# A routing stage rebuilt: squares and weighted rows on TensorE, row arithmetic on GpSimd, row scaling inside the first expert pass

## The chip, the cores and the metric

One NeuronCore of a Trainium2 chip runs the whole program. The metric is the device time of one execution in microseconds (us). Before the change it is 1565.91 us, the median of three runs (1565.65 to 1567.62).

## What is computed

336 tokens (16 meta, 256 prompt, 64 sample) of 1024 channels go through two layers. Each layer is a token mixer followed by a channel mixer; in layer 1 the channel mixer sends every token to two of eight experts:

```
hn = rmsnorm(h, norm2_g)
top_val, top_idx = top_k(hn @ router_w, 2);  gates = softmax(top_val)
y = sum over e of combine[:, e] * ((silu(hn @ wg[e]) * (hn @ wu[e])) @ wd[e])
h = h + y
```

The change lies between the end of the token mixer of layer 1 and the first expert. What has to be known there: the eight router logits of each token, `1/rms` of each token, the two chosen experts, the rank of the token among those of its expert (its row in that expert's chunk of 128 rows), the normalised rows themselves, and the two gates.

## The kernel before

**Layout.** Up to the routing, activations lie with channels on partitions: `h` is 128 x 8 x 336 (eight groups of 128 channels). For the experts, tokens are gathered into chunks of 128 rows. A product of full precision is done as three matmuls in a reduced type (`mm3`, L1571 to L1573) on a high and a low part of both operands. Every weight tile of 1 MB lands in one of six `raw` buffers (SP issues the loads), ScalarE copies it to the high part `w_hi` (L509, "the split"), VectorE subtracts that to get the low part `w_lo` (L514), and TensorE uses both; `w_hi` and `w_lo` have three buffers each, so the split of tile i waits until TensorE is done with tile i-3.

**Output projection of layer 1 (`wout`).** Eight groups of 24 matmuls, two per weight tile; VectorE adds each to `h` (L1321). In between TensorE computes the router's logits of finished channel groups (L1795: three matmuls per channel group, eight columns each), turns the states for output (L1654), and turns `h` to tokens on partitions by transposition (`htok`, L1827: channels 0 to 511 after group 5, the rest after group 7).

**Routing.** VectorE finds the two best experts (L1411 on), `hot` marks them, TensorE sums `hot` over earlier tokens to get ranks (L1882, L1884). ScalarE copies the second half of the turned rows out of PSUM (L999) and sums their squares (L992); VectorE multiplies the rows by the norm's weight (`hn`, L1426) and computes `1/rms` (L1082 on). `sel` (L1443) is the 0/1 matrix of the first expert's rows times `1/rms`; 24 matmuls with `hn` (L1894) gather the first expert's rows straight into PSUM banks `X0`, `X1`; ScalarE and VectorE split those to `xg_hi` (L1013) and `xg_lo` (L1492). For the other seven experts, ScalarE scales all rows by `1/rms` (`hs`, L1006; its buffer shows as `og`), VectorE computes each row's number (L1434 to L1470), and GpSimd scatters the rows to `xg` in DRAM by six indirect DMAs (L734); SP loads each chunk from there in the pass before it is wanted (L573), the first time only after GpSimd's `x_rows`.

**Expert passes.** A loop of eight passes over 42 weight tiles each ("slots"): gate 0 and 1, up 2 and 3, gate of the next block 4 and 5, and so on; 12 matmuls per slot. After slot 1 ScalarE applies Silu (L1031). SP issues the load of slot i when `w_lo` of slot i-6 is done.

What sets the order is the order of the code on each engine, and semaphores between engines. GpSimd's operations of one chain wait for each other (`link`).

Of the kernel before, what the change touches and what calls it, by code (L numbers as in the profile page):

```python
# [22 lines left out]
def hybrid_trunk(nc, x_prompt, x_sample, state_pool, state_conv, meta_tokens, norm1_g, w_in, pool_w,  # L23
# [38 lines left out]

    PE_TAPS = (TAPS, TAPS, TAPS - 1)
# [43 lines left out]
    for l in range(L):  # L107
# [7 lines left out]
        for m in range(KD):  # L115
            plan(("wout", l, m))
            if l == 1 and m == STATE_AFTER:
                plan(*[("state", l, i) for i in range(5)])
            if l == 1 and m in HALF_DONE:

                plan(*[("htok", t, HALF_DONE.index(m)) for t in range(3)])
# [12 lines left out]
    with ExitStack() as ctx:  # L134
# [95 lines left out]
        prod = sb("prod", [TT, 3, 2, NE], F32, moe)  # L230
# [27 lines left out]
        table_load = sb("table_load", [1, 1], F32, moe)  # L258
# [4 lines left out]
        TAP_BANK, N_TAPS = ps[:, 6, 0:L * KC * TAPS], L * KC * TAPS  # L263
        G_, U_, T_, X0, X1 = (ps[:, i, :] for i in (0, 1, 2, 5, 6))
# [32 lines left out]
        gb_landed, hn_sq = sem("gb_landed"), sem("hn_sq")  # L297
# [3 lines left out]
        routed, extra_done = sem("routed"), sem("extra_done")  # L301
# [89 lines left out]


# [127 lines left out]
        def _(sp):  # L520
# [29 lines left out]
            def load_expert(p, e):  # L550
                for j in range(NJ):
# [4 lines left out]
                    for i, w, half, jj in todo:  # L556
# [12 lines left out]
                        if i == gate_slot(2):  # L569
# [38 lines left out]
        def _(pool):  # L608
# [119 lines left out]

            pool.wait_ge(filled, 16 * (2 * CHUNKS + 1))
# [10 lines left out]
            pool.wait_ge(routed, 1)  # L740
# [30 lines left out]
            pool.wait_ge(out_rows_done, 1)  # L771
# [50 lines left out]
        def _(act):  # L822
# [18 lines left out]
            def mixer_layer(l):  # L841
# [153 lines left out]
            token_squares(og[:, 0], [(t, 0) for t in range(3)], lambda t, i: act.wait_ge(evac, GROUP[("htok", t, 0)] + 1), hn_sq)  # L995
            act.wait_ge(evac, GROUP[("htok", 0, 1)])
# [12 lines left out]
            def gathered_hi(p):  # L1009

                for i, x in enumerate((X0, X1)):
                    act.wait_ge(gather_done, p * 2 + (i + 1))
                    nc.scalar.activation(xg_hi[:, 4 * i:4 * i + 4, :], x.rearrange("p (k s) -> p k s", k=4), ACT.Copy  # L1013
                                         ).then_inc(xg_hi_done, 1)
# [8 lines left out]
            def expert_pass(p):  # L1023
# [16 lines left out]
                nc.scalar.activation(table_load[:], ones[0:1, 0:1], ACT.Silu)  # L1040
                for i in range(ES):
                    split_hi_pass(act, p, i)
                    if i == 0:
                        gathered_hi(p)
                    else:
                        after(i - 2)

            with act.Fori(0, NE) as p:
# [16 lines left out]
        def _(dve):  # L1065
# [347 lines left out]
            for t in range(3):  # L1413
# [595 lines left out]
```

## Time and profile before

| | |
|---|---|
| time, median of three | 1565.91 us |
| the profiled execution | 1565.94 us |
| its span (first to last instruction) | 1564.2 us |
| TensorE busy | 1516.5 us (97%) |
| VectorE / ScalarE / GpSimd busy | 1226.7 / 997.5 / 155.4 us |
| HBM traffic | 421.60 MB read, 25.12 MB written |

Times in the views are counted from the span's start. 1.74 us of the profiled execution lie around the span. The output projection of layer 1 ends at about 549 us, the first expert matmul starts at 570.00 us. A "busy" TensorE is one with a matmul in flight: matmuls overlap, so the step from one start to the next says what one costs. A matmul on plain fp32 data shows as two records.

### The profile page before, as it was taken

How to read it: one execution, taken by the hardware profiler on the slowest of the kernel's cores; microseconds unless marked ns; L12 is line 12 of the kernel's file. 1: busy time of each engine (PE TensorE's matmuls, PEld its weight loads, DVE VectorE, ACT ScalarE, POOL GpSimd, SP SyncE). 2: the span in 40 equal slices, each digit the busy share in tenths (PEclk: the TensorE clock that was granted, in tenths of full speed). 3: DMA queues.
4: the chain of work that ended last, by engine and by line, in shares of the span. 5: the costliest groups of instructions: out<-in, count | busy, mean ns of one | idle time of the engine just before them, and what ended most of it. 6: DMA issues, size and time to landing. Idle time of an engine off the chain costs nothing.

```text
span 1564.2 us, 21646 instructions
## 1 busy us (share of the span) xinstructions
PE 1516.5 (97%) x7897; PEld 1321.2 (84%) x7897; DVE 1226.7 (78%) x1053; ACT 997.5 (64%) x1018; POOL 155.4 (10%) x209
## 2 busy tenths in 40 slices
PE   7999999999998989999999999999999999999995
PEld 7989999999998977788888888888888888888884
DVE  4797755544498578888888888888888888888887
ACT  5765343333584267777777777777777778777773
POOL 1036200002122237000000000000000000000002
PEclk9999999999999989999999999999999999999998
DMA  6233998343133449999999999999999999999993
GB/s 194 88 129 115 304 303 253 108 142 128 54 115 108 153 171 394 383 366 392 365 364 386 373 363 379 371 369 382 367 363 372 380 367 366 386 359 367 392 367 105
DMA packets 243536, 447.40 MB, mean 286 GB/s; under 512 B 8901, under 2 KB 93957, under 8 KB 243487
## 3 DMA queue, kind: packets, MB, share of 16 engines
q1 hardware_dynamic: 239296, 436.83, 78.4%
q0 software_dynamic: 2960, 9.73, 2.0%
q8 instruction: 30, 0.49, 0.1%
q10 hardware_dynamic: 1231, 0.19, 0.1%
q14 instruction: 19, 0.16, 0.0%
HBM read 421.60 MB, written 25.12 MB: 286 GB/s over the span
## 4 chain that ended last, share of the span: by engine, by line
issue 57%; PE 4%; POOL 3%; DVE 2%; DMA 2%; ACT 1%; DVEq 0%; POOLq 0%; ACTq 0%
PE ps L1571 1%; PE ps L1573 1%; PE ps L1572 1%; POOL og L767 1%; DMA xg<-og,row_i 1%; POOL h L758 1%; POOL xg L734 0%; DMA h<-last_row 0%; DMA last_row<-last_pos 0%; DMA og<-obuf,out_row_i 0%; POOL pick L754 0%; POOL h L726 0%; DVE scratch L1171 0%; DVE y L1173 0%; PE ps L1795 0%
## 5 line engine op out<-in xcount | busy, mean ns | idle before, releaser
L514 DVE TENSOR_TENSOR w_lo<-raw,w_hi 128x2048 fp32r<-128x2048 f32 x336 | 769.5, 2292 | 126.9 <-ACT w_hi L509 125.3
L509 ACT ACTIVATE w_hi<-raw 128x2048 fp32r<-128x2048 f32 x336 | 643.5, 1916 | 133.9 <-PE ps L1573 122.2
L1571 PE MATMUL ps<-w_hi,xg_hi 128*128 128x512 f32 x896 | 354.9, 396 | 2.5 <-DVE xg_lo L1492 1.6
L1572 PE MATMUL ps<-w_lo,xg_hi 128*128 128x512 f32 x896 | 353.6, 395 | 0.0
L1573 PE MATMUL ps<-w_hi,xg_lo 128*128 128x512 f32 x896 | 353.6, 395 | 0.0
L1571 PEld LDWEIGHTS ps<-w_hi,xg_hi 128*128 128x128 f32 x896 | 168.5, 188 | 43.6 <-DVE xg_lo L1492 1.8
L1573 PEld LDWEIGHTS ps<-w_hi,xg_lo 128*128 128x128 f32 x896 | 168.6, 188 | 40.1
L1572 PEld LDWEIGHTS ps<-w_lo,xg_hi 128*128 128x128 f32 x896 | 168.7, 188 | 39.2
L1571 PE MATMUL ps<-x_hi,w_hi 128*128 128x336 f32 x580 | 187.7, 324 | 10.1 <-DVE x_lo L1117 3.8
L1573 PE MATMUL ps<-x_hi,w_lo 128*128 128x336 f32 x580 | 185.5, 320 | 0.0
L1572 PE MATMUL ps<-x_lo,w_hi 128*128 128x336 f32 x580 | 185.2, 319 | 0.0
L1571 PE MATMUL ps<-w_hi,ft_hi 128*128 128x512 f32 x448 | 181.2, 405 | 0.0
L1573 PE MATMUL ps<-w_hi,ft_lo 128*128 128x512 f32 x448 | 177.1, 395 | 0.0
L1572 PE MATMUL ps<-w_lo,ft_hi 128*128 128x512 f32 x448 | 176.7, 394 | 0.0
L502 DVE TENSOR_TENSOR w_lo<-raw,w_hi 128x2048 fp32r<-128x2048 f32 (+3 forms) x41 | 85.1, 2079 | 55.3 <-ACT w_hi L484 53.9
L1571 PEld LDWEIGHTS ps<-x_hi,w_hi 128*128 128x128 f32 x580 | 110.6, 191 | 14.2 <-issue 6.1
L1572 PEld LDWEIGHTS ps<-x_lo,w_hi 128*128 128x128 f32 x580 | 110.7, 191 | 0.3
L1573 PEld LDWEIGHTS ps<-x_hi,w_lo 128*128 128x128 f32 x580 | 110.4, 190 | 0.0
L484 ACT ACTIVATE w_hi<-raw 128x2048 fp32r<-128x2048 f32 (+3 forms) x41 | 70.1, 1719 | 53.7 <-PE ps L1573 53.7
L1573 PEld LDWEIGHTS ps<-w_hi,ft_lo 128*128 128x128 f32 x448 | 84.2, 188 | 19.7
L767 POOL DMA_INDIRECT og<-obuf,out_row_i x6 | 11.5, 1920 | 889.2 <-SPq L595 887.7
L1572 PEld LDWEIGHTS ps<-w_lo,ft_hi 128*128 128x128 f32 x448 | 84.5, 189 | 17.6
(275 smaller groups left out, 1871.2 us busy)
## 6 DMA issues: line engine op xcount, KB each, us to landing
raw<-in_moe_w_gate_dram SPq DMA_DIRECT2D x112, 1024.0 KB, 7.6
raw<-in_moe_w_up_dram SPq DMA_DIRECT2D x112, 1024.0 KB, 7.9
raw<-in_moe_w_down_dram SPq DMA_DIRECT2D x112, 1024.0 KB, 7.5
raw<-in_w_in_dram SPq DMA_DIRECT2D x11, 1024.0 KB, 5.0
raw<-in_ffn_w_gate_dram SPq DMA_DIRECT2D x11, 1024.0 KB, 5.9
raw<-in_ffn_w_up_dram SPq DMA_DIRECT2D x11, 1024.0 KB, 6.4
raw<-in_w_out_dram SPq DMA_DIRECT2D x8, 1024.0 KB, 5.1
obuf<-ones SPq DMA_DIRECT2D x15, 512.0 KB, 7.9
```

The lines of the kernel that those rows point to most:

```text
L484: nc.scalar.activation(hi, r, ACT.Copy).then_inc(hi_done, 1)
L502: nc.vector.tensor_tensor(lo, r, hi.bitcast(F32), ALU.subtract).then_inc(lo_done, 1)
L509: nc.scalar.activation(hi, r, ACT.Copy).then_inc(hi_done, 1)
L514: nc.vector.tensor_tensor(lo, r, hi.bitcast(F32), ALU.subtract).then_inc(lo_done, 1)
L758: link(nc.gpsimd.tensor_tensor(pick_e[:, i, NE * c:NE * (c + 1)], pick[:, i, NE * c:NE * (c + 1)], iota_e[:], ALU.mult))
L767: nc.gpsimd.indirect_dma_start(out=og[:, i, t, :], out_offset=None, in_=obuf, in_offset=bass.IndirectOffsetOnAxis(ap=out_row_i[:, i, t:t + ...
L1571: nc.tensor.matmul(out, a_hi, b_hi, start=start, stop=False)
L1572: nc.tensor.matmul(out, a_hi, b_lo, start=False, stop=False)
L1573: return nc.tensor.matmul(out, a_lo, b_hi, start=False, stop=stop)
```

## The change

On TensorE the squares of a channel group, made by ScalarE in its channel layout, are summed over channels by matmuls with a column of ones, three for each of eight channel groups, beside the logits of the same group. The logits of groups 4 and 5 move ahead of the last output group. The second half of `hn` comes from matmuls of `h` with a diagonal matrix of the norm's weight in place of a transposition and a VectorE product; the transposition of the second half stays (the residual needs it) and moves behind the ranks. Four matmuls on constants stand ahead of the gather. ScalarE loads the table for Exp by a one-element instruction ahead of the wait for the gap; the scaling of all rows (`hs`) leaves the routing and stands in pass 0 between the Silu of slot 1 and the split of slot 4; pass 0 is written out and the loop runs over the other seven. Its split of the gathered rows comes one half per slot. The row numbers and the ordering of the two gates go from VectorE to GpSimd, which gets a copy of the ranks in SBUF. On SP, the store of a finished chunk and the load of the next chunk both stand after slot 16, the store first; before, the load stood after slot 10.

TensorE, from the end of the last output group to the first expert matmul, before (`rwg` is the router's weight, `ident` the identity: transposition):

```order
L1573 MATMUL ps<-m_hi,w_lo 128x336
L1795 MATMUL ps<-rwg,h 112x8 x12
L1827 MATMUL ps<-ident,h 112x128 x12
L1882 MATMUL ps<-hot,before 128x32
L1884 MATMUL ps<-hot,ones 128x24
L1884 MATMUL ps<-hot,ones 128x16
L1884 MATMUL ps<-hot,ones 128x8
L1894 MATMUL ps<-sel,hn 128x128 x24
```

and in the changed kernel (`y_pool` holds squares, `z` the diagonal of the weight):

```order
L1603 MATMUL ps<-m_hi,w_lo 128x336
L1835 MATMUL ps<-rwg,h 112x8 x6
L1843 MATMUL ps<-ones,y_pool 112x1 x6
L1874 MATMUL ps<-z,h 112x128 x12
L1677 MATMUL ps<-hot,before 128x32
L1679 MATMUL ps<-hot,ones 128x24
L1679 MATMUL ps<-hot,ones 128x16
L1679 MATMUL ps<-hot,ones 128x8
L1886 MATMUL ps<-ident,h 112x128 x12
L1638 MATMUL ps<-ones,ident 128x128 x4
L1947 MATMUL ps<-sel,hn 128x128 x24
```

Squares and the product with the diagonal stand ahead of the ranks, the transposition behind them; six of the twelve logits matmuls have moved ahead of the last output group, where TensorE now has:

```order
L1835 MATMUL ps<-rwg,h 112x8 x3
L1843 MATMUL ps<-ones,y_pool 112x1 x3
L1835 MATMUL ps<-rwg,h 112x8 x3
L1843 MATMUL ps<-ones,y_pool 112x1 x3
L1601 MATMUL ps<-m_hi,w_hi 128x336
```

The same kind of block stands at the two earlier places, where before six logits matmuls stood.

ScalarE, from its last copies out of the turned rows into the first pass, before:

```order
L999 ACTIVATE yt<-ps 112x512 [waits mm_done] x2
L992 ACTIVATE og,nt<-yt 112x512 [waits evac] x3
L1006 ACTIVATE og<-hn,nt 112x1024 [waits hn_done,gap_done]
L1006 ACTIVATE og<-hn,nt 112x1024 [waits hn_done] x2
L1007 ACT_TABLE_LOAD
L1007 ACTIVATE gt<-gt 112x3
L1048 UNCONDITIONAL_BRANCH
L1040 ACT_TABLE_LOAD
L1040 ACTIVATE table_load<-ones 1x1
```

and in the changed kernel, the routing's end and then the place of the row scaling:

```order
L1065 ACTIVATE yt<-ps 112x512 [waits mm_done] x2
L1067 ACT_TABLE_LOAD
L1067 ACTIVATE table_load<-ones 1x1
L1069 ACTIVATE gt<-gt 112x3 [waits gap_done]
L1100 ACT_TABLE_LOAD
L1100 ACTIVATE table_load<-ones 1x1
L520 ACTIVATE w_hi<-raw 128x2048 [waits w_used,landed0]
```

```order
L520 ACTIVATE w_hi<-raw 128x2048 [waits w_used,landed3]
L1091 ACTIVATE act_s<-ps 128x512 [waits e_f,g_done]
L1111 ACTIVATE og<-hn,nt 112x1024 [waits hn_done]
L1111 ACTIVATE og<-hn,nt 112x1024 x2
L520 ACTIVATE w_hi<-raw 128x2048 [waits g_done,landed4]
```

The three scalings have moved from ahead of the table loads to between the Silu of slot 1 and the split of slot 4.

The diff's core:

```diff
+
+        def squared(k):
+            return scratch[:, k, :] if k < 4 else y_pool[:, k - 4, :]
...
-                        if i == gate_slot(2):
+                        if i == gate_slot(3):
+
+                            sp.wait_ge(o_done, p * 2 + 2)
+                            sp.dma_start(obuf_chunks[ds(p, 1)].rearrange("a p d -> p (a d)"), o[:]
+                                         ).then_inc(o_stored, 16)
...
-                        if i == gate_slot(3):
-
-                            sp.wait_ge(o_done, p * 2 + 2)
-                            sp.dma_start(obuf_chunks[ds(p, 1)].rearrange("a p d -> p (a d)"), o[:]
-                                         ).then_inc(o_stored, 16)
...
+            def fold_experts(x, out):
+
+                for n in (4, 2, 1):
+                    link(nc.gpsimd.tensor_tensor(x[:, :, 0:n], x[:, :, 0:n], x[:, :, n:2 * n], ALU.add))
+                link(nc.gpsimd.tensor_copy(out, x[:, :, 0]))
+
+            def pick_expert(out, values):
+                link(nc.gpsimd.tensor_tensor(prod[:].rearrange("p (t k) e -> p t k e", t=3), hot2[:], values, ALU.mult))
+                fold_experts(prod, out[:].rearrange("p t k -> p (t k)"))
+
+            pool.wait_ge(ranks_copied, 1)
+            pick_expert(rank, ranks_sb[0:TT, 0:3].unsqueeze(2).broadcast_to([TT, 3, 2, NE]))
...
+            fold_experts(before_e, key_e[:])
+            link(nc.gpsimd.tensor_scalar(key_e[:], key_e[:], float(P), None, ALU.mult))
+            link(nc.gpsimd.tensor_tensor(key_e[:], key_e[:], extra_base[:], ALU.add))
+            pick_expert(jump, key_e[0:TT].unsqueeze(1).unsqueeze(1).broadcast_to([TT, 3, 2, NE]))
...
+            link(nc.gpsimd.tensor_tensor(row[:], row[:], jump[:], ALU.add))
+            nc.gpsimd.tensor_copy(row_i[:], row[:]).then_inc(rows_done, 1)
...
+            pool.wait_ge(gates_done, 1)
+            first_row, gap, step_up = row[:, :, 0], last_pos[:], early_gate[:]
+            link(nc.gpsimd.tensor_tensor(gap, first_row, row[:, :, 1], ALU.subtract))
...
+            link(nc.gpsimd.tensor_copy(out_row_i[:], out_row[:]))
+            pool.sem_inc(out_rows_done, 1)
...
+                        continue
+                    if s == 0:
+                        act.wait_ge(evac, GROUP[("wout", 1, 0)] + 1)
+                        for k in range(4):
+                            nc.scalar.activation(z[:, k, P:2 * P], ident[:], ACT.Copy, scale=col(1, NG2, 4 + k)
+                                                 ).then_inc(gain_done, 1)
+                    for k in (2 * s, 2 * s + 1):
+                        act.wait_ge(evac, GROUP[("wout", 1, k)] + 1)
+                        nc.scalar.activation(squared(k), h[:, k, :], ACT.Square).then_inc(h_sq, 1)
...
-            token_squares(og[:, 0], [(t, 0) for t in range(3)], lambda t, i: act.wait_ge(evac, GROUP[("htok", t, 0)] + 1), hn_sq)
-            act.wait_ge(evac, GROUP[("htok", 0, 1)])
+            act.wait_ge(evac, GROUP[("hn", 0)])
+            for t in range(3):
+                act.wait_ge(mm_done, GROUP[("hn", t)] + 1)
+                nc.scalar.activation(hn[:, t, 512:1024], ps[0:TT, GROUP[("hn", t)] % MM_BANKS, :], ACT.Copy
+                                     ).then_inc(hn_turned, 1)
+                act.wait_ge(hn_turned, t + 1)
+                act.sem_inc(evac, 1)
...
-            token_squares(og[:, 0], [(t, 1) for t in range(3)], lambda t, i: act.wait_ge(evac, GROUP[("htok", t, 1)] + 1), hn_sq)
-
+            nc.scalar.activation(table_load[:, 1:2], ones[0:1, 0:1], ACT.Exp)
             act.wait_ge(gap_done, 1)
-            for t in range(3):
-                act.wait_ge(hn_done, 3 + t + 1)
-                nc.scalar.activation(hs[:, t, :], hn[:, t, :], ACT.Copy, scale=nt[0:TT, t, 1:2]).then_inc(hn_scaled, 1)
             nc.scalar.activation(gt[:, :, 1], gt[:, :, 0], ACT.Exp).then_inc(exp_done, 1)
 
...
+                    if i < 2:
+                        gathered_hi(p, i)
...
+                    if i == rows_at:
+
+                        act.wait_ge(hn_done, 3)
+                        for t in range(3):
+                            nc.scalar.activation(hs[:, t, :], hn[:, t, :], ACT.Copy, scale=nt[0:TT, t, 1:2]
+                                                 ).then_inc(hn_scaled, 1)
+
+            expert_pass(0, ROWS_AT)
+            with act.Fori(1, NE) as p:
...
+            dve.wait_ge(squares_done, 1)
+            link(nc.vector.tensor_scalar(nt[0:TT, :, 0], SQUARE_SUMS, 1.0 / D, 1e-6, ALU.mult, ALU.add))
             nc.vector.tensor_tensor(hot[:, 0:3], hot2[:, :, 0, :], hot2[:, :, 1, :], ALU.add).then_inc(hot_done, 1)
             dve.wait_ge(hot_done, 2)
...
-            for t in range(3):
-                dve.wait_ge(evac, GROUP[("htok", t, 1)] + 1)
-                nc.vector.tensor_tensor(hn[:, t, 512:1024], yt[:, t, 512:1024], gb[:, 0, 512:1024], ALU.mult
-                                        ).then_inc(hn_done, 1)
-            dve.wait_ge(hn_sq, 6)
-            rstd_tokens()
-            link(nc.vector.tensor_tensor(gt[:, :, 0], top[:, :, 1], top[:, :, 0], ALU.subtract))
...
+            rsqrt(nt[0:TT, :, 0], nt[0:TT, :, 1], nt[0:TT, :, 2], nt[0:TT, :, 3])
...
+            link(nc.vector.tensor_tensor(gt[:, :, 0], top[:, :, 1], top[:, :, 0], ALU.subtract))
+            nc.vector.tensor_tensor(gt[:, :, 0], gt[:, :, 0], nt[0:TT, :, 1], ALU.mult).then_inc(gap_done, 1)
+            nc.vector.tensor_copy(ranks_sb[:].rearrange("p t e -> p (t e)"), ps[:, 7, 0:4 * NE]).then_inc(ranks_copied, 1)
...
-            pick_expert(rank, ps[0:TT, 7, 0:3 * NE].rearrange("p (t e) -> p t e", t=3).unsqueeze(2)
-                        .broadcast_to([TT, 3, 2, NE]))
...
-            nc.vector.tensor_copy(row_i[:], row[:]).then_inc(rows_done, 1)
-
-            dve.sem_inc(routed, 1)
...
+            nc.vector.tensor_tensor(gt[:, :, 3], gt[:, :, 1], gt[:, :, 2], ALU.mult).then_inc(gates_done, 1)
...
+                def token_squares(k):
+
+                    pe.wait_ge(h_sq, k + 1)
+                    for t in range(3):
+                        ins = nc.tensor.matmul(SQUARE_SUMS[:, t:t + 1], squared(k)[:, TT * t:TT * (t + 1)],
+                                               ones[:, 0:1], start=(k == 0 and t == 0), stop=(k == KD - 1 and t == 2))
+                    return ins
...
+                        if l == 1 and s and i == (0 if s == 3 else 1):
+                            for k in (2 * s - 2, 2 * s - 1):
+                                logits(k)
+                                token_squares(k)
                     m = 2 * s + 1
-                    if l == 1 and s:
-                        for k in (m - 3, m - 2):
-                            logits(k)
                     if l == 1 and m == KD - 1:
                         logits(KD - 2)
                         logits(KD - 1).then_inc(logits_done, 1)
+                        token_squares(KD - 2)
+                        token_squares(KD - 1).then_inc(squares_done, 1)
+                        pe.wait_ge(gain_done, 4)
+                        for t in range(3):
+                            out = group(("hn", t))
+                            for k in range(4):
+                                ins = nc.tensor.matmul(out[0:TT, P * k:P * (k + 1)], h[:, 4 + k, TT * t:TT * (t + 1)],
+                                                       z[:, k, P:2 * P], start=True, stop=True)
+                            ins.then_inc(mm_done, 1)
+                        ranks()
                     if l == 1 and m == STATE_AFTER:
...
-            pe.wait_ge(hn_done, 6)
+            keep_busy(WARM_ROUTE, 6)
+            pe.wait_ge(hn_done, 3)
+            pe.wait_ge(hn_turned, 3)
             pe.wait_ge(sel_ready, 3)
```

## Rows read from the trace of the kernel before

**Rows 1.** Timeline of TensorE: start us, us, engine, line, operation, count [idle before <-releaser].
```profile
549.18 2.43 PE L1795 MATMUL ps<-rwg,h 128*112 128x8 f32 x24
551.47 1.79 PE L1827 MATMUL ps<-ident,h 128*112 128x128 f32 x12
553.69 1.43 PE L1884 MATMUL ps<-hot,ones 112*128 112x24 f32 x6
559.64 8.72 PE L1894 MATMUL ps<-sel,hn 112*128 112x128 f32 x48 [4.53 <-DVE sel L1443]
570.00 0.50 PE L1571 MATMUL ps<-w_hi,xg_hi 128*128 128x512 f32 x1 [1.64 <-DVE xg_lo L1492]
```

**Rows 2.** Windows: stretch, PE PEld DVE ACT POOL busy, granted clock, DMA, GB/s.
```profile
700.00:1500.00 800.00, 800.00 (x3565) 649.30 (x3564) 695.95 (x384) 596.03 (x407) 0.00 (x0) 1.00 1.02 372
```

**Rows 3.** Waits of TensorE from 569 to 700 us: total, times, longest.
```profile
PE ps L1571 <- DVE xg_lo L1492: 1.6, 1, 1.6
PE ps L1571 <- DVE w_lo L514: 0.9, 3, 0.4
```

**Rows 4.** Timeline of TensorE in layer 0: sums over channels of one column.
```profile
110.65 2.43 PE L1768 MATMUL ps<-ones,z 128*112 128x1 f32 x24
```

**Rows 5.** Timeline of VectorE around the routing and the first slots.
```profile
549.38 0.51 DVE L1321 TENSOR_TENSOR h<-h,ps 128x336 f32<-128x336 f32 x1 [3.20 <-PE ps L1573]
567.05 2.29 DVE L514 TENSOR_TENSOR w_lo<-raw,w_hi 128x2048 fp32r<-128x2048 f32 x1
569.26 1.28 DVE L1492 TENSOR_TENSOR xg_lo<-ps,xg_hi 128x512 fp32r<-128x512 f32 x2
578.77 4.61 DVE L514 TENSOR_TENSOR w_lo<-raw,w_hi 128x2048 fp32r<-128x2048 f32 x2 [1.07 <-ACT w_hi L509]
```

**Rows 6.** Windows of the gather (L1894) alone: PE, PEld busy, clock, DMA, GB/s.
```profile
560.00:564.00 4.00, 4.00 (x20) 4.00 (x20) 0.50 0.00 0
566.20:568.40 2.20, 2.16 (x19) 1.97 (x18) 1.00 0.64 199
```

**Rows 7.** Timeline of ScalarE: scaling, table loads, splits.
```profile
558.36 3.23 ACT L1006 ACTIVATE og<-hn,nt 112x1024 f32<-112x1024 f32 x3 [2.64 <-DVE gt L1431]
561.61 1.28 ACT L1007 ACT_TABLE_LOAD   x1
564.53 1.89 ACT L509 ACTIVATE w_hi<-raw 128x2048 fp32r<-128x2048 f32 x1
576.83 1.91 ACT L509 ACTIVATE w_hi<-raw 128x2048 fp32r<-128x2048 f32 x1
```

**Rows 8.** Timeline of TensorE: first matmuls of slots 1 and 4.
```profile
573.25 0.49 PE L1571 MATMUL ps<-w_hi,xg_hi 128*128 128x512 f32 x1 [0.21 <-DVE w_lo L514]
581.72 0.39 PE L1571 MATMUL ps<-w_hi,xg_hi 128*128 128x512 f32 x1
```

**Rows 9.** Windows: the granted clock (ahead of DMA) at four places.
```profile
57.60:61.00 3.40, 3.40 (x17) 3.40 (x16) 3.29 (x4) 2.40 (x2) 0.00 (x0) 0.50 0.00 0
61.00:64.40 3.40, 3.40 (x28) 3.40 (x27) 3.29 (x5) 0.34 (x1) 0.00 (x0) 1.00 0.48 140
528.60:531.80 3.20, 3.20 (x33) 3.10 (x32) 1.96 (x4) 0.00 (x0) 0.46 (x1) 1.00 0.02 9
552.50:566.20 13.70, 9.17 (x44) 8.71 (x43) 10.87 (x50) 10.99 (x17) 0.96 (x1) 0.50 0.01 2
```

**Rows 10.** Timeline of GpSimd: scatter and first arithmetic.
```profile
565.24 1.05 POOL L734 DMA_INDIRECT xg<-og,row_i  x1 [29.45 <-DVE row_i L1470]
583.47 0.58 POOL L742 TENSOR_SCALAR over<-cnt 128x8 f32<-128x8 f32 x2 [7.34 <-DMA xg<-og,row_i]
584.14 2.15 POOL L743 TENSOR_TENSOR n_chunks<-over 128x8 f32<-128x8 f32 x1
```

**Rows 11.** Timeline of SP: the load of slot 16.
```profile
598.01 0.37 SPq L568 DMA_DIRECT2D raw<-in_moe_w_gate_dram  x1
```

**Rows 12.** The page's DMA issues: KB each, median us to landing.
```profile
raw<-in_moe_w_gate_dram SPq DMA_DIRECT2D x112, 1024.0 KB, 7.6
```

More of the change, by code:

```diff
@@ L61, in hybrid_trunk @@
     WARM = (12, 10)
+    WARM_ROUTE = 4
+    ROWS_AT = 3
     PE_TAPS = (TAPS, TAPS, TAPS - 1)
@@ L119, in hybrid_trunk @@
             if l == 1 and m in HALF_DONE:
+                if m == KD - 1:
+                    plan(*[("hn", t) for t in range(3)])
                 plan(*[("htok", t, HALF_DONE.index(m)) for t in range(3)])
@@ L296, in hybrid_trunk @@
         state_stored = sem("state_stored")
-        gb_landed, hn_sq = sem("gb_landed"), sem("hn_sq")
+        gb_landed, h_sq, gain_done = sem("gb_landed"), sem("h_sq"), sem("gain_done")
+        squares_done, ranks_copied, gates_done, hn_turned = (
+            sem(n) for n in ("squares_done", "ranks_copied", "gates_done", "hn_turned"))
         rwg_done, logits_done, hot_done, ranks_done = sem("rwg_done"), sem("logits_done"), sem("hot_done"), sem("ranks_done")
@@ L769, in gather_outputs @@
                     in_offset=bass.IndirectOffsetOnAxis(ap=out_row_i[:, i, t:t + 1], axis=0)).then_inc(done, 16)
-            pool.wait_ge(out_rows_done, 1)
+            pool.wait_ge(gates_done, 1)
+            first_row, gap, step_up = row[:, :, 0], last_pos[:], early_gate[:]
+            link(nc.gpsimd.tensor_tensor(gap, first_row, row[:, :, 1], ALU.subtract))
+            for i, under in enumerate((ALU.is_lt, ALU.is_ge)):
+                link(nc.gpsimd.tensor_scalar(lower[:, i, :], gap, 0.0, None, under))
+            link(nc.gpsimd.tensor_tensor(step_up, gap, lower[:, 0, :], ALU.mult))
+            link(nc.gpsimd.tensor_tensor(out_row[:, 0, :], row[:, :, 1], step_up, ALU.add))
+            link(nc.gpsimd.tensor_tensor(out_row[:, 1, :], first_row, step_up, ALU.subtract))
+            for i in (0, 1):
+                link(nc.gpsimd.tensor_tensor(out_gate[:, i, :], lower[:, i, :], gt[:, :, 2], ALU.mult))
+                link(nc.gpsimd.tensor_tensor(part_gate[:, i, :], lower[:, 1 - i, :], gt[:, :, 3], ALU.mult))
+            link(nc.gpsimd.tensor_tensor(out_gate[:], out_gate[:], part_gate[:], ALU.add))
+            link(nc.gpsimd.tensor_scalar(out_row[:], out_row[:], float(P), None, ALU.add))
+            link(nc.gpsimd.tensor_copy(out_row_i[:], out_row[:]))
+            pool.sem_inc(out_rows_done, 1)
             link(nc.gpsimd.tensor_scalar(last_base[:], eids_f[0:TT, 6:7], -float(P), -float(P * NE), ALU.mult, ALU.add))
@@ L1513, in expert_pass @@
                     split_lo_pass(dve, p, i)
-                    if i == 0:
-                        gathered_lo(p)
+                    if i < 2:
+                        gathered_lo(p, i)
                     else:
@@ L1603, in spread, with keep_busy @@
                 nc.tensor.matmul(SUM_BANK, ones[0:TT, :], spread_in, start=True, stop=True).then_inc(sums_done, 1)
-            def keep_busy(n):
+            def keep_busy(n, bank=7):
                 for _ in range(n):
-                    nc.tensor.matmul(ps[:, 7, 0:P], ident[:], ones[:], start=True, stop=True)
+                    nc.tensor.matmul(ps[:, bank, 0:P], ident[:], ones[:], start=True, stop=True)
             pe.wait_ge(consts, 1)
@@ L1641, in split_ready, with ranks @@
                 pe.wait_ge(lo_done, n + 1)
+            def ranks():
+                pe.wait_ge(hot_done, 2)
+                flat = hot[:].rearrange("p t e -> p (t e)")
+                nc.tensor.matmul(ps[:, 7, 0:4 * NE], before[0:TT, :], flat, start=True, stop=False)
+                for t in range(3):
+                    ins = nc.tensor.matmul(ps[:, 7, NE * (t + 1):4 * NE].rearrange("p (u e) -> p u e", e=NE), ones[0:TT, :],
+                                           hot[:, t, :].unsqueeze(1).broadcast_to([TT, 3 - t, NE]), start=False, stop=t == 2)
+                ins.then_inc(ranks_done, 1)
             def turn_states(l):
@@ L1818, in mixer_layer @@
                         logits(KD - 1).then_inc(logits_done, 1)
+                        token_squares(KD - 2)
+                        token_squares(KD - 1).then_inc(squares_done, 1)
+                        pe.wait_ge(gain_done, 4)
+                        for t in range(3):
+                            out = group(("hn", t))
[4 more added lines that the diff above has]
+                        ranks()
                     if l == 1 and m == STATE_AFTER:
@@ L1877, in _ @@
             mixer_layer(1)
-            pe.wait_ge(hot_done, 2)
-            flat = hot[:].rearrange("p t e -> p (t e)")
-            nc.tensor.matmul(ps[:, 7, 0:4 * NE], before[0:TT, :], flat, start=True, stop=False)
-            for t in range(3):
-                ins = nc.tensor.matmul(ps[:, 7, NE * (t + 1):4 * NE].rearrange("p (u e) -> p u e", e=NE), ones[0:TT, :],
-                                       hot[:, t, :].unsqueeze(1).broadcast_to([TT, 3 - t, NE]), start=False, stop=t == 2)
-            ins.then_inc(ranks_done, 1)
-            pe.wait_ge(hn_done, 6)
+            keep_busy(WARM_ROUTE, 6)
+            pe.wait_ge(hn_done, 3)
+            pe.wait_ge(hn_turned, 3)
             pe.wait_ge(sel_ready, 3)
```

72 lines of the change are left out of this document (26 added, 46 removed).

## The prediction

> **What bounds the kernel now.** I read the timeline of TensorE first, between the last group of the output projection and the first expert matmul [rows 1]. The last group ends at 549.18 us, the experts start at 570.00: 20.8 us in which TensorE does little and waits twice, for `sel` (4.53) and for `xg_lo` (1.64). Next the windows behind it: from 700 to 1500 us TensorE is busy in 800.00 of 800 us at full clock [rows 2]; from 569 to 700 its waits come to 1.6 us (`xg_lo`) and 0.9 us (three for `w_lo`, the longest 0.4) [rows 3]. So the experts run at TensorE's pace; what moves the first expert matmul, or adds a wait of TensorE in pass 0, moves the end by as much. The chain of waits at the page's end names other engines; it follows semaphores back and does not say which engine has no time left, so I don't use it.
>
> **TensorE ahead of the last output group.** The squares of six channel groups are 18 matmuls on plain data, 36 records; 12 logits records move to here. A one-column matmul costs what an eight-column one does: 24 records take 2.43 us in layer 0 [rows 4] and 2.43 for the logits [rows 1]. From start to start that is (551.47 - 549.18)/24 = 0.095 us. 48 x 0.095 = **+4.6 us**, all of it between output groups that depend on nothing else, so on the path. The rule that speaks otherwise is in the Trainium skill, "TensorE: Matmul & The Clock Gate", "Back-to-back issue gap": matmuls of up to 64 columns come some 25 ns apart. By it (an estimate) the 48 would take 1.2 us and the sum below would be 3.4 lower. The same page, "LDWEIGHTS", has a weight load take its columns divided by 1.2 in ns, 93 ns at 112 columns, and with that the 0.095 of this trace agrees.
>
> **The tail after that group.** I count from 549.18 + 4.6 = 553.8. Logits of group 6: 0.57. Group 7's wait for VectorE's addition, which in before ends 549.38 + 0.51 - 549.18 = 0.7 us after the group [rows 5]; its logits, to 1.3. Squares of groups 6 and 7, 12 x 0.095, to 2.5. The product with the diagonal has the shape of the gather, 24 records; the gather alone shows 19 records in 2.16 us at full clock, 0.114 each, and 20 in 4.00 at half, 0.2 each [rows 6]. So 2.7, to 5.2. Ranks: 8 records, 0.9, to 6.1. Transposition of 12: between 12 x 0.114 = 1.4 and the 1.79 seen; 1.5, to 7.6. From here ScalarE carries the path: the last copy (half of one 1024-wide scaling, 3.23/3/2 = 0.54) to 8.1; two table loads with their small instructions, which in before last from 561.61 to 564.53, 2.9, and one more small one, 3.0 in all, to 11.1; the split of a weight tile, 1.89, to 13.0 [rows 7]. Then VectorE: `w_lo` 2.29 and half of the two `xg_lo`, 0.64 [rows 5], to 16.0. First expert matmul at 553.8 + 16.0 = 569.8, 0.2 earlier than before. Slot 1 in before waits for `w_lo` until 573.25 [rows 8]; the changed kernel makes that `w_lo` ahead of slot 0, so slot 1 starts near 572.9. I take **-0.3** for both. The gather comes at some 8.5, lasts 48 x 0.114 = 5.5, and is done at 14, ahead of `w_lo`'s end, so its four matmuls on constants cost nothing; that cover ends 2 us later. Bounds: -1.2 if the copy and the small instructions hide beside TensorE, up to +4.1 through the clock.
>
> **The clock.** TensorE's granted clock has two levels, 1.2 and 2.4 GHz. Behind the narrow matmuls and the transposition it is 0.50 of full from 552.5 to 566.2; in layer 0, work that waits runs at 0.50 with 17 records in 3.40 us where 28 fit later at 1.00; 12 narrow records beside transpositions at 528.6 to 531.8 stayed at 1.00 [rows 9]. The changed kernel has four stretches of 24 narrow records, three of them inside the output projection. One stay like the one at 57.6 in full-size matmuls costs 3.40 x (1 - 17/28) = 1.3 us. Nothing of before shows 24 narrow records inside running products, so the cost lies between 0 and, for three stays, 3.9; alternatively the tail runs at half clock: the diagonal product 24 x 0.086 = 2.1, ranks 1.0, transposition 1.0, together 4.1. I take one stay, **+1.3**.
>
> **The row scaling in pass 0.** In before ScalarE splits slot 4 at 576.83 to 578.74 [rows 7], VectorE subtracts from 578.77 to 578.77 + 4.61/2 = 581.07 [rows 5], TensorE wants it at 581.72 [rows 8]: 0.65 us to spare. Three scalings, 3.23 us [rows 7], now stand in front of that split, behind a Silu that itself waits for TensorE. So TensorE waits 3.23 - 0.65 = **+2.6 us** at slot 4. Behind it ScalarE needs 1.9 a slot against TensorE's 2.82 and catches up at once, and all demand is 2.3 us later, while the landings of the weights are not: of the 0.9 us of `w_lo` waits, those after slot 1 (0.9 - 0.2) go, **-0.6**, at worst 0.
>
> **Off the path, costed at nothing.** The chain for the row numbers (27 operations on GpSimd) can start near 562, once the ranks (553.8 + 6.1) are copied and VectorE's `sel` is through; its GpSimd form takes 0.29 us an operation (two in 0.58), and beside a `w_lo` of VectorE 2.15 [rows 10]. The first 14 (0.35 each with a gap) end near 567, before VectorE is loaded again; 13 more at 0.4 to 2.2 end between 572 and 596. The scatter then takes 583.47 - 565.24 = 18.2 us [rows 10], so the rows are there between 598 and 615 (the scaling, done near 580, gives 598 too). SP wants them where the load of the next chunk now stands, behind the load of slot 16, which it asks for at 598.01 [rows 11] + 2.3 = 600.3. Queued behind that wait are the loads of slot 17 on; TensorE goes from slot 1 to slot 4 in 581.72 - 573.25, 2.82 a slot, and comes to slot 17 near 581.7 + 2.3 + 13 x 2.82 = 621, so with 7.6 to land [rows 12] and 4.2 for split and subtraction SP may wait until 609. The Trainium skill, "GPSIMD Engine Reference", "Performance versus the Vector engine", has plain arithmetic about twice as slow there as on VectorE. By it the chain would take some 11 us (an estimate) and SP would not wait; the 2.15 us of the trace is worse than this, and only through it does the rival below have a chance. SP's store of a finished chunk now stands ahead of that wait and is off the path. GpSimd's gate arithmetic serves the end of the kernel, far behind. The VectorE operations that go stood in the 20.8 us, and the path there is counted anew.
>
> **Sum.** -0.3 + 1.3 + 2.6 - 0.6 = +3.0 on the profiled 1565.94: **1568.9**. That this lies 0.03 above the median of the runs is nothing. Of the parts, +4.6 is paid in full by what the tail saves; the gain on paper is spent ahead of it.
>
> **Rivals.**
> 1. *No stay at half clock.* The 528.6 window speaks for it, the 552.5 one against. +1.7: 1567.6.
> 2. *The tail at half clock*, as from 552.5 in before, beside the terms without the stay: 1.7 + 4.1 = +5.8: 1571.7. For it: the same narrow stretch precedes the tail; against: the wait in it is shorter.
> 3. *The row numbers come late*: GpSimd beside VectorE as in the 2.15 us row, all 13 times, SP held until 615: 6 more than the forecast, 1575. It decides if the chain ends after 591; against: VectorE has gaps in pass 0.
> 4. *The scaling is hidden; not slower.* The place is slot 4: if the split of slot 4 is done within its spare 0.65 us (the scalings lie beside a wait that ScalarE has there anyway, as Silu waits for TensorE, or a late landing decides the time of that split), TensorE doesn't wait: -0.9 to +0.4, 1565.0 to 1566.3, and with a start at the bound of -1.2 below 1562.8 when the stays are missing and the narrow records overlap the output groups' weight loads.
> 5. *The 48 narrow records cost 1.2 us*, by the rule named: +3.0 - 3.4, 1565.5; with rival 4 below 1562.8.
>
> **How the numbers follow.** A difference of 0.2%, 3.1 us, is about what a measurement of this kernel can tell from none: the bounds are 1562.8 and 1569.0. Chances: forecast 0.36 (own range 1567.3 to 1570.3; 0.19 of it same, 0.17 slower), rival 1 0.22 (0.20 same, 0.02 slower), rival 2 0.19 (slower), rival 3 0.04 (slower), rival 4 0.15 (0.06 faster, 0.09 same), rival 5 0.04 (0.03 faster, 0.01 same). Together faster 0.09, same 0.49, slower 0.42. The range 1564.3 to 1573.0 leaves out the lower part of rivals 4 and 5 and the upper one of 2 and 3.
>
> **What would show it.** Right: the first expert matmul near 569.8; a wait of TensorE of 2.6 us for `w_lo` at slot 4, with the three scalings between Silu and split on ScalarE; one-column records 0.095 apart; one window at 0.50 among the output groups from 520 to 554; no waits for `w_lo` after slot 4; SP's load of slot 17 behind no wait. Wrong: the diagonal product at 0.2 a record (rival 2), slot 4 on time (rival 4), TensorE waiting near slot 17 with SP held by GpSimd (rival 3).

## The result, and the profile after

The changed kernel takes 1573.06 us, median of seven runs (1572.42 to 1575.13), against 1566.67 us of the kernel before, also of seven (1564.02 to 1568.76). The ratio is 1.0042, with an interval of 1.0032 to 1.0052: 6.4 us slower. A second set of twelve runs beside 35 of before gave 1.0034 (1.0022 to 1.0046). Forecast were 1568.9 us, 3.0 more than before, and a range that ended at 1573.0, with a chance of 0.42 for slower, 0.49 for the same and 0.09 for faster. The sign was right; the loss was about twice the forecast's.

The profiled execution has a span of 1572.2 us, 8.0 more than before. Below, the tail is the stretch from the end of the last output group to the first expert matmul, and a stay is a stretch of some microseconds in which the granted clock is 0.50, the lower of its two levels. The timeline of TensorE in the tail, and the first matmul of slot 4:

```profile
556.22 1.52 PE L1835 MATMUL ps<-rwg,h 128*112 128x8 f32 x12
557.59 1.58 PE L1843 MATMUL ps<-ones,y_pool 128*112 128x1 f32 x12
559.03 4.25 PE L1874 MATMUL ps<-z,h 128*112 128x128 f32 x24
563.93 1.50 PE L1886 MATMUL ps<-ident,h 128*112 128x128 f32 x12
566.16 5.52 PE L1947 MATMUL ps<-sel,hn 112*128 112x128 f32 x48
574.08 0.50 PE L1601 MATMUL ps<-w_hi,xg_hi 128*128 128x512 f32 x1 [2.39 <-DVE xg_lo L1521]
589.41 0.79 PE L1601 MATMUL ps<-w_hi,xg_hi 128*128 128x512 f32 x1 [2.37 <-DVE w_lo L525]
```

Against [rows 1] the tail is shorter, 17.9 us (556.22 to 574.08) for 20.8; the wait for `sel` (4.53 us before) is gone, and the gather takes 5.52 us for 8.72. The tail begins later, though, and the diagonal product takes 4.25 us where 2.7 were forecast. The wait for `xg_lo` is still there, longer than before, and slot 4 has a wait that it did not have [rows 8]. The waits of TensorE from 520 to 700 us, where before had 4.5 for `sel`, 1.6 for `xg_lo` and three for `w_lo` of together 0.9 [rows 1, rows 3]:

```profile
PE ps L1601 <- DVE xg_lo L1521: 2.4, 1, 2.4
PE ps L1601 <- DVE w_lo L525: 2.4, 1, 2.4
```

Windows of the same execution (TensorE, weight loads, VectorE, ScalarE, GpSimd busy, then the granted clock): the output projection, the diagonal product, what follows it, the matmuls behind each of the two waits, and the late passes of [rows 2]:

```profile
516.00:556.20 40.20, 40.20 (x298) 40.09 (x297) 18.24 (x24) 10.76 (x16) 5.21 (x10) 1.00 0.38 125
558.70:562.10 3.40, 3.40 (x18) 3.40 (x19) 2.19 (x13) 0.60 (x1) 0.00 (x0) 0.53 0.00 0
562.10:566.10 4.00, 4.00 (x39) 4.00 (x38) 1.52 (x8) 2.70 (x5) 0.17 (x1) 1.00 0.01 2
575.60:578.90 3.30, 3.30 (x9) 2.63 (x8) 3.30 (x3) 1.48 (x4) 3.05 (x4) 0.50 1.02 366
589.40:592.60 3.20, 3.19 (x8) 2.52 (x9) 3.20 (x3) 1.23 (x1) 2.66 (x2) 0.50 0.48 90
700.00:1500.00 800.00, 800.00 (x3562) 649.28 (x3561) 695.46 (x383) 590.28 (x404) 0.00 (x0) 1.00 1.01 372
```

The late passes are untouched. There are three stays, and none is in the output projection, where the forecast had put its one. ScalarE, the end of the routing and the place of the scaling, to set beside [rows 7]:

```profile
566.19 1.28 ACT L1067 ACT_TABLE_LOAD   x1
567.80 1.28 ACT L1100 ACT_TABLE_LOAD   x1
569.20 1.89 ACT L520 ACTIVATE w_hi<-raw 128x2048 fp32r<-128x2048 f32 x1
582.01 3.22 ACT L1111 ACTIVATE og<-hn,nt 112x1024 f32<-112x1024 f32 x3
585.13 5.50 ACT L520 ACTIVATE w_hi<-raw 128x2048 fp32r<-128x2048 f32 x3
```

GpSimd, beside [rows 10]: the row numbers are ready before the scaled rows, and the scatter waits 6.14 us for ScalarE.

```profile
579.80 0.19 POOL L766 CAST row_i<-row 112x6 int32<-112x6 f32 x1
586.13 1.10 POOL L773 DMA_INDIRECT xg<-og,row_i  x1 [6.14 <-ACT og L1111]
604.94 2.56 POOL L780 TENSOR_SCALAR over<-cnt 128x8 f32<-128x8 f32 x2 [7.29 <-DMA xg<-og,row_i]
```

So the 8.0 us of the spans: 2.3 lie ahead of the change (the output projection begins at 513.74 before and 516.04 after); the projection takes 35.4 and 40.2 us (+4.74); the tail 20.8 and 17.9 (-2.96); and from the first expert matmul to the 240th matmul on gathered rows behind it 82.2 and 86.2 (+4.0). The last three sum to +5.8 us, between the 6.4 and the 5.3 (0.34% of 1567.8) of the timed sets.

### The profile page after: what moved, and what is told of

Read it like the earlier page. It is cut to its first block, busy times and chain, and to the rows that moved or that the text cites. A ratio compares the mean times of both kernels' runs of the same rounds, so it can differ in the third digit from the quotient of the medians.

```text
span 1572.2 us, 21802 instructions
## 1 busy us (share of the span) xinstructions
PE 1527.5 (97%) x7977; PEld 1332.8 (85%) x7977; DVE 1221.3 (78%) x1025; ACT 991.5 (63%) x1015; POOL 189.5 (12%) x249
## 4 chain that ended last, share of the span: by engine, by line
issue 55%; PE 5%; POOL 5%; DVE 2%; DMA 2%; ACT 1%; POOLq 0%; DVEq 0%; ACTq 0%
PE ps L1601 1%; PE ps L1603 1%; PE ps L1602 1%; POOL h L796 1%; POOL og L805 1%; POOL xg L773 1%; DMA xg<-og,row_i 1%; POOL key L784 0%; DMA h<-last_row 0%; DMA last_row<-last_pos 0%; DMA og<-obuf,out_row_i 0%; POOL pick L792 0%; PE ps L1843 0%; DVE scratch L1238 0%; DVE y L1240 0%
```

## The experiments

The theory: the terms that were forecast are there, and to them come stays in the diagonal product and behind each of the two waits of TensorE. Its rivals: the loss lies in code ahead of the change, or late landings decide. All ratios are to the kernel before, timed beside each; an interval of 0.1% either way is 1.6 us, so what a stay costs is read from the profiles and not from the times.

**The scaling on VectorE.**

```diff
-                    if i == rows_at:
-                        act.wait_ge(hn_done, 3)
-                        for t in range(3):
-                            nc.scalar.activation(hs[:, t, :], hn[:, t, :], ACT.Copy, scale=nt[0:TT, t, 1:2]
...
+            def scaled(t):
+                dve.wait_ge(hn_done, 3)
+                dve.wait_ge(hn_turned, t + 1)
+                nc.vector.tensor_scalar(hs[:, t, :], hn[:, t, :], nt[0:TT, t, 1:2], None, ALU.mult).then_inc(hn_scaled, 1)
+            scaled(0)
...
+            scaled(1)
+            scaled(2)
```

> The changed kernel, but VectorE scales the rows by 1/rms, in the time it has between the ranks and the first expert (one tile ahead of the ranks' wait, two behind the gates), and ScalarE's three scalings in pass 0 are gone. Theory (the wait of TensorE at slot 4, 2.37 us in the changed kernel's trace, comes from the 3.22 us of scaling, and the half-clock matmuls from 589 to 593, some 1.5 us, come from that wait): TensorE does not wait at slot 4, its clock stays at 1.00 there, and the time is 3.9 us under the changed kernel's 1573.1: 1569.2. Rival one (the wait goes, but the clock falls there anyway): 2.4 us, 1570.7. Rival two (a late landing decides slot 4): the wait stays, named for the DMA, under 1 us gained.

Ratio 1.0020 (1.0007 to 1.0032), 2.2 to 3.5 us below the changed kernel's 1.0042 and 1.0034 in its own two sets: less than the 3.9 expected, and rival one's 2.4 fits too. The waits of TensorE from 569 to 700 us, and the window 575 to 579:

```profile
PE ps L1603 <- DVE xg_lo L1523: 2.4, 1, 2.4
PE ps L1603 <- DVE w_lo L525: 0.2, 1, 0.2
575.00:579.00 4.00, 3.94 (x17) 3.15 (x18) 4.00 (x4) 3.38 (x4) 3.78 (x4) 1.00 0.82 269
```

The wait at slot 4 is gone and nothing late took its place (the 0.2 us stand at 624), so rival two falls. No stay stands there either (1.00 from 575 to 600), so in this profile rival one falls too. The third row shows something else: behind the same wait for `xg_lo` the clock stayed at 1.00 this time. In this profile two stays came in the output projection instead, which took 43.3 us in place of 40.2; in the other five profiles of kernels with all 48 narrow records there it took 40.1 or 40.2.

**Table loads off the path.**

```diff
+            nc.scalar.activation(table_load[:, 1:2], ones[0:1, 0:1], ACT.Exp)
             act.wait_ge(evac, GROUP[("hn", 0)])
...
-            nc.scalar.activation(table_load[:, 1:2], ones[0:1, 0:1], ACT.Exp)
             act.wait_ge(gap_done, 1)
...
-                nc.scalar.activation(table_load[:, 0:1], ones[0:1, 0:1], ACT.Silu)
+                if rows_at is None:
+                    nc.scalar.activation(table_load[:, 0:1], ones[0:1, 0:1], ACT.Silu)
...
+                        if i == 1 and rows_at is not None:
+                            nc.scalar.activation(table_load[:, 0:1], ones[0:1, 0:1], ACT.Silu)
```

> The changed kernel, but ScalarE loads the table for Exp ahead of its copies out of the turned rows, where it waits for TensorE anyway, and the one for Silu behind the split of slot 1. Theory (between the last copy and the first split two table loads and three small instructions, 3.0 us, stand on the path; without them TensorE begins the experts right behind the gather): the wait for xg_lo, 2.39 us, goes to under 0.3, the half-clock matmuls from 575.5 to 579, 1.1 us, go with it, and the time is 3.5 us under the changed kernel's: 1569.6. Rival one (only the wait goes): 2.4, 1570.7. Rival two (a copy under the table of Exp loads another table, or the split waits for something else): no gain.

Ratio 1.0019 (1.0007 to 1.0031), 2.4 to 3.6 us below the changed kernel's; expected were 3.5, and the 2.4 of the wait alone fit as well. ScalarE, and then the waits of TensorE from 530 to 700 us:

```profile
570.81 0.22 ACT L1069 ACTIVATE gt<-gt 112x3 f32<-112x3 f32 x1
570.91 1.92 ACT L520 ACTIVATE w_hi<-raw 128x2048 fp32r<-128x2048 f32 x1
577.11 1.28 ACT L1107 ACT_TABLE_LOAD   x1
```

```profile
PE ps L1604 <- DVE w_lo L525: 2.9, 2, 2.3
```

The first split follows the small Exp at once, the tail is 15.3 us in place of 17.9, and the wait for `xg_lo` is gone. One of the two waits left is slot 4's, 2.3; the other, 0.56, is new, at slot 2, where the load for Silu now stands ahead of the split. The theory holds for the table loads. That the clock is at 1.00 behind the first expert matmul here says little, as it was so in two of the five profiles that kept the wait.

**Wide sums.**

```diff
-        SQUARE_SUMS = ps[0:TT, 7, 4 * NE:4 * NE + 3]
+        SQUARE_COLS = ps[0:TT, 7, 64:64 + 3 * 64]
+        SQUARE_SUMS = SQUARE_COLS.rearrange("p (t c) -> p t c", c=64)[:, :, 0]
...
-                        ins = nc.tensor.matmul(SQUARE_SUMS[:, t:t + 1], squared(k)[:, TT * t:TT * (t + 1)],
-                                               ones[:, 0:1], ...
+                        ins = nc.tensor.matmul(SQUARE_COLS[:, 64 * t:64 * (t + 1)], squared(k)[:, TT * t:TT * (t + 1)],
+                                               ones[:, 0:64], ...
```

> The changed kernel, but every sum of squares is made 64 times over (a matmul with 64 columns of ones in place of one). Theory (the diagonal product ran at half clock, 4.25 us where 2.7 was forecast, because of what TensorE did right before it, and a matmul of 64 columns costs no more time than one of one): the product takes 2.7 us at clock 1.00 and the time is 1.4 us under the changed kernel's: 1571.7. Rival one (the clock does not follow the matmuls' columns): the product stays at 4.2 us, same time. Rival two (the 48 matmul records get longer): up to 1 us slower.

Ratio 1.0029 (1.0020 to 1.0039). The diagonal product, its window, and the window behind the wait for `xg_lo`:

```profile
557.79 2.83 PE L1875 MATMUL ps<-z,h 128*112 128x128 f32 x24
557.80:560.40 2.60, 2.60 (x26) 2.60 (x26) 2.10 (x13) 1.19 (x2) 0.00 (x0) 1.00 0.02 6
571.50:574.50 3.00, 3.00 (x7) 2.39 (x8) 3.00 (x3) 2.43 (x3) 2.75 (x4) 0.50 0.79 253
```

From its start to the ranks the product takes 2.67 us for 4.09. In the eight profiles with one-column sums it took 4.06 to 4.29, in the three with wide ones 2.66 or 2.67: this stay is no chance, and the columns of the sums right ahead of the product decide it, as nothing else was changed. Rival two falls: the projection takes 40.1 us with 64 columns as with one. The stay behind the wait for `xg_lo` is back here. The interval alone can't tell 1.4 us from nothing; the profiles do.

**Matmuls on constants in the wait.**

```diff
+    WARM_GATHERED = 10
...
                 ins.then_inc(gather_done, 1)
+            pe.wait_ge(ranks_copied, 1)
+            keep_busy(WARM_GATHERED, 7)
```

> The changed kernel with ten matmuls on constants (2.2 us) between the gather and the first expert matmul, where TensorE waited 2.39 us for xg_lo. Theory (the half clock from 575.5 to 579 follows from that wait): the first expert matmul comes when it did, the clock stays at 1.00 through slots 0 and 1, and the time is 1.1 us under the changed kernel's: 1572.0. Rival (the clock falls for another reason, or the wait is harmless): within 0.3 us of the changed kernel.

Ratio 1.0028 (1.0015 to 1.0041). The window behind the first expert matmul (at 577.05, 17.85 us after the last group, as in the changed kernel):

```profile
577.00:580.00 3.00, 2.94 (x13) 2.32 (x14) 3.00 (x4) 2.59 (x3) 2.69 (x5) 1.00 0.80 243
```

The clock is at 1.00, as expected. But of the five profiles with an unfilled wait of 2.39 us it was at half in three, so one filled profile is no proof. The time, 0.9 to 2.2 us below the changed kernel's of the two other sets, can't tell the expected 1.1 from nothing. Inconclusive.

**The changed kernel again.**

> The changed kernel itself, beside the next ones on one chip. Theory (the stays at half clock in the diagonal product, behind the wait for xg_lo and behind slot 4 belong to the change; those ahead of 513 us come and go from run to run and hit both kernels): in the profile the diagonal product takes 4.2 us again, TensorE waits 2.4 us at slot 4, at least one of the stretches behind the two waits is at half clock, and the ratio to before lies at 1.0030 to 1.0045. Rival (the 2.5 us by which the first profile was behind at 513 us are part of the change): the output projection begins 2 to 3 us late again.

Ratio 1.0034 (1.0022 to 1.0046). Diagonal product 4.10 us, both waits of the first profile (2.39 and 2.37), and a stay behind each; the windows of the product and of the two:

```profile
558.00:561.50 3.50, 3.50 (x20) 3.50 (x20) 1.98 (x12) 0.60 (x2) 0.00 (x0) 0.58 0.00 0
574.60:578.00 3.40, 3.40 (x10) 2.62 (x8) 3.40 (x3) 1.60 (x4) 3.15 (x4) 0.50 1.01 371
588.40:591.60 3.20, 3.16 (x8) 2.48 (x9) 3.20 (x3) 1.26 (x1) 2.69 (x2) 0.50 0.59 93
```

The projection begins at 515.09, not late by 2 to 3 us; over all twelve profiles, of kernels with the same code up to there, it begins between 512.09 and 521.30. The rival falls: what differs ahead of the change differs from run to run.

**Squares added up by GpSimd.**

```diff
+            for k in (0, 1, 2, 3, 5, 6):
+                pool.wait_ge(h_sq, max(k, 4) + 1)
+                link(nc.gpsimd.tensor_tensor(squared(4), squared(4), squared(k), ALU.add))
+                if k in (3, 6):
+                    pool.sem_inc(sq_summed, 1)
...
                                 logits(k)
-                                token_squares(k)
...
-                        token_squares(KD - 2)
+                        pe.wait_ge(sq_summed, 2)
+                        token_squares(4)
```

> The changed kernel, but GpSimd adds the squares of seven channel groups in its idle time, and TensorE sums two arrays over channels in place of eight: 12 one-column records remain of 48. Theory (each record costs 0.095 us, in the output projection too): 36 x 0.095 = 3.4 us less between the first and the last output group, 36.8 us in place of 40.2, and 3.4 us less in all. Rival one (records of one column cost 0.025 us): 0.9 us less. Rival two (GpSimd's additions are late for the tail): the sums wait, up to 3 us lost again.

Ratio 1.0005 (0.9994 to 1.0017), 4.7 us under the changed kernel in the same set; expected were 3.4. GpSimd's additions, the first four and the last, ahead of the tail that begins at 550.85:

```profile
537.39 3.86 POOL L752 TENSOR_TENSOR y_pool<-y_pool,scratch 128x336 f32<-128x336 f32 x4 [1.14 <-ACT y_pool L1011]
547.31 0.91 POOL L752 TENSOR_TENSOR y_pool<-y_pool 128x336 f32<-128x336 f32 x1 [4.98 <-ACT y_pool L1011]
```

The output projection takes 36.63 us in place of 40.18: 3.55 us for 36 records, 0.099 each. The forecast's 0.095 stands, and rival one's 0.025 falls. The Trainium skill ("TensorE: Matmul & The Clock Gate", "LDWEIGHTS (loading the stationary operand)") divides a weight load's columns by 1.2 to get ns, 93 ns for 112 columns as an estimate, and this trace agrees within 6 ns, with 99 ns a record. The 25 ns for 1 to 64 columns in the Trainium skill, same page, "Back-to-back issue gap", are given there for the isolated gap of a single matmul, and that section says that in a stream of weight loads and matmuls both set the spacing; these records are such a stream, so the 25 ns don't apply to them.

Neither wait of this profile (2.39 and 2.35 us) was followed by a stay; the windows behind them:

```profile
568.70:573.00 4.30, 4.29 (x18) 3.42 (x19) 4.30 (x3) 3.69 (x4) 3.98 (x5) 1.00 0.88 278
582.50:586.00 3.50, 3.50 (x17) 2.88 (x18) 3.50 (x3) 1.22 (x1) 2.89 (x3) 1.00 0.52 119
```

That fits a gain above the 3.4, but it is one profile.

**Three edits together** (scaling, tables, GpSimd's sums), and the same **with wide sums**.

> Three edits together: scaling on VectorE, table loads off the path, squares added up by GpSimd. Theory (the parts add up: 3.9 + 3.7 + 3.4 = 11.0 us under the changed kernel): 4 to 5 us under the kernel before, ratio 0.997 to 0.9975; TensorE waits nowhere between the gather and slot 10 over 0.6 us. Rival (VectorE, which now has the scaling in the time that the shorter tail takes away, is late with the first w_lo): the wait for xg_lo or w_lo at slots 0 and 1 comes back with 1 to 2 us and the ratio is 0.998 to 0.999.

> The last kernel with sums of squares 64 columns wide. Theory (wide matmuls keep the clock in the tail): the diagonal product at 2.7 us and clock 1.00, 1.4 us under the kernel with three edits, ratio to before 0.996 to 0.9965. Rival (the clock falls in the tail through the waits in it): same time as with three edits.

The ratios are 0.9979 (0.9968 to 0.9991) and 0.9984 (0.9971 to 0.9998): with three edits 3.3 us under the kernel before, where 4 to 5 were expected. The wide sums, which were to bring 1.4 us more, don't show in the time, though their profile has the diagonal product at 2.66 us for 4.16. The waits of TensorE (560 to 700 us) and one of SP (570 to 640 us) with three edits:

```profile
PE ps L1614 <- DVE w_lo L526: 1.7, 1, 1.7
PE ps L1614 <- DVE xg_lo L1534: 1.1, 1, 1.1
```

```profile
SPq L589 <- POOLq L784: 9.3, 1, 9.3
```

Here SP is held as in rival 3 of the prediction, but not by late numbers. They are ready at 582.0, where that rival asked for 591; the experts start at 565.28, 8.8 us earlier than in the changed kernel, so that SP stands at the load of the next chunk for 9.3 us, until 603.5, while the scatter ends. TensorE then waits 1.73 us at 616.17 (1.81 with wide sums, with matmuls at half clock behind it). The expected rival, VectorE late at slots 0 and 1, shows as 1.1 us.

**The load of the next chunk later**, with and without wide sums.

```diff
+                        if i == gate_slot(4):
                             sp.wait_ge(x_rows, 1)
                             sp.wait_ge(gather_done, p * 2 + 2)
```

> The kernel with three edits, and SP asks for the next chunk of rows behind the load of slot 22 in place of slot 16. Theory (in the kernel with three edits SP waited 9.3 us for the scattered rows with the loads of slot 17 on queued behind, and TensorE then waited 1.73 us for w_lo near 616): no such wait, 1.7 us less, and up to 1.5 more where half clock followed it; ratio to before 0.9965 to 0.997. Rival (the landings near 616 are late anyway, as in the kernel before, whose waits there came to 0.7 us): 1 us less at most.

> The same with sums of squares 64 columns wide. Theory: the diagonal product at clock 1.00 and no wait of SP for the rows: ratio to before 0.9955 to 0.9965. Rival (what the clock gives in the tail is lost in a longer wait for xg_lo, since ScalarE and VectorE set the first expert matmul): same as the kernel without the wide sums.

The ratios are 0.9968 (0.9956 to 0.9981, eleven runs), as expected, and 0.9947 (0.9930 to 0.9965, six runs, median 1560.83 against 1567.24), a little lower than expected. With one-column sums a wait of 0.63 us for `w_lo` is left near 622; with wide ones TensorE waits once from 560 to 700 us, and the clock is full in the tail and behind the wait:

```profile
PE ps L1616 <- DVE xg_lo L1536: 1.2, 1, 1.2
```

```profile
554.00:558.00 4.00, 4.00 (x39) 4.00 (x39) 3.21 (x17) 2.34 (x5) 0.00 (x0) 1.00 0.03 6
566.80:600.00 33.20, 33.20 (x147) 26.91 (x148) 30.00 (x17) 26.03 (x20) 28.23 (x21) 1.00 0.99 362
```

The wait of SP is gone in both. Of the 1.7 to 1.8 us that TensorE then waited, 0.63 and nothing are left, so SP's wait made most of it, and late landings, the rival, at most the rest. The version with wide sums beats both kernels. How far its lead over the one-column version (2.4 us of the medians; the intervals overlap) is the tail and how far luck with the stays, these runs don't settle.

## Why the prediction was right in direction and wrong in size

- *What bounds the kernel.* Right: what the marks up to 660 us lose comes out at the end (2.3 + 4.74 - 2.96 + 4.0 = 8.1, for 8.0 of the spans); 700 to 1500 us is the same in both profiles.
- *TensorE ahead of the last group, +4.6.* Right: +4.74, and taking 36 of the 48 records out again gave 3.55 back.
- *The tail, -0.3.* Wrong by its size. Forecast were 16.0 us, measured 17.9: the diagonal product at half clock (+1.4, a matter of the clock, below), the squares of the last two channel groups (done at 2.8 us where 2.5 was forecast, +0.3) and the last copy out of the turned rows (0.9 for 0.54, +0.4), against small gains. The order on the path was as forecast, table loads and first split included: moving the loads took the wait for `xg_lo` away.
- *The row scaling, +2.6.* Right: 2.37 us at slot 4, gone when VectorE scales.
- *The other waits for `w_lo`, -0.6.* Right: from 575 to 700 us none is left but slot 4's.
- *Off the path, at nothing.* Right: the chain for the row numbers ended at 580.0, inside the 572 to 596 that were forecast, and SP did not wait for it.
- *The clock, +1.3.* This is the step that failed: "I take one stay", priced inside the output projection. In the profiled execution there were three, none of them there, of together 4.2 us: 1.4 in the diagonal product and two behind the waits. Those two cover 3.30 and 3.20 us at 0.50, 8 and 6 matmul steps of 0.43 us for 0.23, 1.6 and 1.2 us. The stay in the tail happened in all eight profiles with one-column sums and in none of the three with wide ones. The prediction had set it against its one stay as a rival of 0.19, and that the misplaced 1.3 and the real 1.4 are alike is luck. Missing in the sum are the other two. The prediction forecast both waits, 2.6 us at slot 4 and some 2 us between the end of the gather and the first expert matmul, but priced them by their length alone, though what followed them cost half to two thirds as much again.
- *What ties these stays to the waits.* A stay came behind the 2.39 us in three of five profiles and behind slot 4 in four of six; behind the shorter waits of this stretch, 0.2 to 1.8 us, it came once, behind one of 1.81. In all twelve profiles, windows of 1 us over the 110 us from the first expert matmul on show no other stay: without a wait there was none, but not every wait brought one. What decides in the single case these runs don't show, and as filling the wait settled nothing, that the wait is the cause rests on this count.
- *The sum.* 3.0 as forecast, less the 1.3 misplaced, plus 1.4 + 0.7 - 0.2 in the tail and 2.8 behind the waits: 6.4, beside 5.8 from the profile's marks, 6.4 and 5.3 from the timed sets. Part of the difference to 5.8 is in the waits of before, which cost more than their 0.9 us: the step into the waiting matmul at 573.25 [rows 8] is 0.60 us and the one after it 0.33, where two steps of 0.23 are usual, 0.47 us for a wait of 0.21.
- *Rivals.* Rival 2 was half of the truth, without the ranks and the transposition that it counted: after 562.1 the clock was back. That its 5.8 is the 5.8 of the marks is luck, as it has neither the two stays behind the waits nor the 0.7 of the tail. Rival 3 did not occur in the changed kernel, as the numbers were ready at 580.0 and the scatter waited for the scaling. Rivals 1, 4 and 5 are refuted.

## What to carry to other kernels

Price a new wait of TensorE in a saturated stretch with its length and, as a likely extra, a stay at half clock behind it (here 1.2 to 1.6 us behind waits of 2.3 to 2.4, in seven of eleven cases); look in the trace of before for what TensorE's clock does behind each existing wait and each run of narrow matmuls. Work moved out of a stall into a saturated loop is only free if its engine has that much time ahead of the next hand-over: compare the spare at that one hand-over (0.65 us here) with the whole piece (3.2), not the engine's average load. When an earlier start has been won, look at once for what was timed by the old start: here the scattered rows, on which the queue of weight loads then stood for 9.3 us.

## What the runs showed that was not expected

The same code ahead of the change ends 9.2 us apart in two executions. One stretch of layer 0 in the kernels with three edits, without and with wide sums:

```profile
106.00:131.00 25.00, 23.20 (x151) 21.97 (x152) 19.94 (x43) 15.19 (x26) 12.07 (x19) 1.00 0.52 169
```

```profile
106.00:131.00 25.00, 22.18 (x107) 20.10 (x108) 18.64 (x35) 10.66 (x18) 9.34 (x14) 0.73 0.39 127
```

Nothing in the code differs there; the granted clock does, and the same 25 us hold 151 matmul records in one and 107 in the other. From 20 to 511 us the clock is 0.99 and 0.97. What sets it off is open. With it fits that timed runs of one kernel scatter over 8 us (1564.12 to 1572.06 for the kernel before in one set); a difference of a few microseconds is better read from marks within the changed stretch than from two spans.

VectorE scales a tile of 112 x 1024 in 0.75 us, ScalarE in 1.08 (3.23 for three in [rows 7]). Copies on ScalarE behind a table load for Exp brought no further one (none from 562.23 to 577.11 us in the run with the loads moved). On GpSimd three of the 27 operations for the row numbers took over 2 us beside a `w_lo`, as [rows 10] suggested, without harm here.
